# Five edits to a fused transformer kernel: DVE takes half of the modulation, one ada row moves into the MLP, four bias buffers, two score pairs ahead, ScalarE spreads the reciprocals

## The reference

```python
for i in range(2):
    mod = silu(c) @ ada_w[i] + ada_b[i]          # six rows of 1024: sh1, sc1, g1, sh2, sc2, g2
    mod_c = silu(c_ctx) @ ada_w[i] + ada_b[i]    # the same for the 256 context tokens
    h, hc = x * (1 + sc1) + sh1, ctx * (1 + sc1c) + sh1c
    y, yc = retention(h, hc) if i == 0 else neighbourhood(h, hc)
    x = layer_norm(alpha * x + g1 * y)           # ctx alike, in layer 0 only
    h = x * (1 + sc2) + sh2
    x = layer_norm(alpha * x + g2 * (relu(h @ mlp_w1[i]) ** 2 @ mlp_w2[i]))

# neighbourhood attention of layer 1: 32 heads of width 32, 256 queries, 256 local and 256 context keys
s = concat([q @ k_local.T + bias[head], q @ k_ctx.T])
o = softmax(s) @ v
```

## Time and profile before

| | us |
|---|---|
| median of three runs | 2924.24 |
| the profiled execution | 2926.24 |
| its span on the core | 2924.2 |
| PE busy in the span | 2752.2 (94%) |
| DVE busy | 1892.6 (65%) |
| ACT busy | 566.0 (19%) |
| POOL busy | 125.4 (4%) |

### The profile page before, as it was taken

One profiled execution on the slowest core, in us unless ns is written; L12 is line 12 of the kernel. 1 busy time (PEld: TensorE's weight loads), 2 busy tenths in 40 slices (PEclk: granted clock), 3 DMA queues, 4 the chain that ended last, 5 costly groups with the idle time before them and its releaser, 6 DMA issues.

```text
span 2924.2 us, 34915 instructions
## 1 busy us (share of the span) xinstructions
PE 2752.2 (94%) x13475; PEld 2209.9 (76%) x13475; DVE 1892.6 (65%) x2173; ACT 566.0 (19%) x1224; POOL 125.4 (4%) x118
## 2 busy tenths in 40 slices
PE   5999999799997997899899999999989999999998
PEld 3777776577776764789688877788878887878887
DVE  3455456455437357787776968587677687766766
ACT  2111110311111135212110231311020013131101
POOL 0000000000001002200000001010000000000100
PEclk8999999899998998999999999699999999978999
DMA  6332422344334443455454535155455454433643
GB/s 244 130 110 78 158 101 87 97 135 167 140 107 124 145 123 73 131 188 189 155 175 169 163 129 172 45 184 182 147 192 184 166 168 139 158 102 101 203 160 136
DMA packets 251850, 420.65 MB, mean 144 GB/s; under 512 B 35576, under 2 KB 93376, under 8 KB 251680
## 3 DMA queue, kind: packets, MB, share of 16 engines
q1 hardware_dynamic: 247824, 410.09, 42.9%
q0 software_dynamic: 2720, 5.14, 0.6%
q10 hardware_dynamic: 1136, 3.12, 0.3%
HBM read 417.27 MB, written 1.05 MB: 143 GB/s over the span
## 4 chain that ended last, share of the span: by engine, by line
PE 60%; issue 28%; DVE 5%; DMA 2%; POOL 2%; ACT 1%; SPq 1%; ACTq 0%; POOLq 0%; DVEq 0%
PE psum L406 57%; PE psum L420 2%; POOL small L1872 2%; DVE wgt_lo L1291 1%; SPq L1963 1%; DMA W<-nat_rpb 1%; DVE wgt_hi L1289 1%; DMA raw<-ada_w 1%; ACT psum L916 1%; ACT xh L916 0%; DMA raw<-nat_w_in 0%; DMA raw<-mlp_w 0%; POOL W L1912 0%; PE psum L627 0%; ACT W L916 0%
## 5 line engine op out<-in xcount | busy, mean ns | idle before, releaser
L1291 DVE TENSOR_TENSOR wgt_lo<-raw,wgt_hi 128x2048 fp32r<-128x2048 f32 (+2 forms) x352 | 776.1, 2205 | 12.1
L406 PE MATMUL psum<-wgt_hi,xh 128*128 128x512 f32 (+2 forms) x1824 | 704.3, 386 | 13.3 <-DVE wgt_lo L1291 8.0
L406 PE MATMUL psum<-wgt_lo,xh 128*128 128x512 f32 (+2 forms) x1824 | 695.3, 381 | 0.0
L406 PE MATMUL psum<-wgt_hi,xl 128*128 128x512 f32 (+2 forms) x1824 | 695.2, 381 | 0.0
L1289 DVE CAST wgt_hi<-raw 128x2048 fp32r<-128x2048 f32 (+2 forms) x352 | 415.5, 1180 | 334.2 <-PE psum L406 122.3
L406 PEld LDWEIGHTS psum<-wgt_hi,xh 128*128 128x128 f32 x1824 | 346.9, 190 | 93.1 <-issue 20.2
L406 PEld LDWEIGHTS psum<-wgt_hi,xl 128*128 128x128 f32 x1824 | 346.6, 190 | 66.5
L406 PEld LDWEIGHTS psum<-wgt_lo,xh 128*128 128x128 f32 x1824 | 346.8, 190 | 64.8 <-issue 1.0
L406 PE MATMUL psum<-wgt_hi,yh 128*128 128x512 f32 x944 | 371.8, 394 | 7.5 <-DVE wgt_lo L1291 4.9
L406 PE MATMUL psum<-wgt_hi,yl 128*128 128x512 f32 x944 | 367.8, 390 | 0.0
L406 PE MATMUL psum<-wgt_lo,yh 128*128 128x512 f32 x944 | 367.6, 389 | 0.0
(11 more groups left out here) (172 smaller groups left out, 2059.9 us busy)
## 6 DMA issues: line engine op xcount, KB each, us to landing
raw<-mlp_w SPq DMA_DIRECT2D x64, 1024.0 KB, 5.3
raw<-w_in SPq DMA_DIRECT2D x60, 1024.0 KB, 5.0
raw<-ada_w SPq DMA_DIRECT2D x48, 1024.0 KB, 7.3
raw<-ffn_w_gate SPq DMA_DIRECT2D x40, 1024.0 KB, 5.1
raw<-ffn_w_up SPq DMA_DIRECT2D x40, 1024.0 KB, 5.1
raw<-ffn_w_down SPq DMA_DIRECT2D x40, 1024.0 KB, 5.0
raw<-ret_w_in SPq DMA_DIRECT2D x24, 1024.0 KB, 5.3
raw<-nat_w_in SPq DMA_DIRECT2D x12, 1024.0 KB, 5.3
```

The costliest lines, as they stand in the source:

```text
L406: return pe.matmul(o, l, r, start=start_, stop=stop, skip_group_check=True)
L1291: v.tensor_tensor(wgt_lo[:, s % RING, :size], r, wgt_hi[:, s % RING, :size], ALU.subtract).then_inc(split_done.sem, split_done.up())
```

## The change

1. `low_x2` replaces `low_x` for `h0`, `h0m` and `h1`: DVE scales and shifts every odd tile in PSUM (two `tensor_scalar` of 128x256), ahead of the subtraction for the even tile before it; ACT only copies the odd tiles.
2. The four `ada_w` blocks of row 4 of layer 1 move from `nk` into the last chunk of the MLP of layer 0; those of row 5 move from `nv` to `nk`. The transposes that turn the rows into columns move along.
3. Four bias buffers in place of two. The two new ones lie in `x_rest`, which shares its memory with `xl`, so biases 2 and 3 are loaded after the last `nv` product; bias b from 4 on is loaded after the row minima of bias b-4.
4. Scores, row minimum and exponentials of pair 1 come before `nv` as well, like those of pair 0.
5. The reciprocals are still taken by DVE; ACT spreads them (`nat_spread`), after the exponentials of every fourth pair.

```diff
@@ PE, mlp()
+                    more_up, more_down = ({0: 0, 2: 1}, {2: 2, 3: 3}) if layer == 0 and c == 3 else ({}, {})
-                                       after=lambda b: b in in_up and modulation(1, c, in_up[b]),
+                                       after=lambda b: (b in in_up and modulation(1, c, in_up[b]), b in more_up and modulation(1, 4, more_up[b])),
...
+                    if more_up:
+                        modulation_columns(1, 4)
@@ PE, attention
-            features_by_tokens("nk", D, KT, 2 * T, "act", wb, after=lambda b: modulation(1, 4, b))
+            features_by_tokens("nk", D, KT, 2 * T, "act", wb, after=lambda b: modulation(1, 5, b))
             nat_scores(0)
-            tokens_by_features("nv", KT, 2 * D, D, range(4), x_op(xh), x_op(xl), "act", wb,
-                               after=lambda b: (modulation(1, 5, b), b == 0 and modulation_columns(1, 4)))
+            nat_scores(1)
             modulation_columns(1, 5)
+            tokens_by_features("nv", KT, 2 * D, D, range(4), x_op(xh), x_op(xl), "act", wb)
@@ ACT, operand_x()
-                    if streams == 2:
+                    if streams == 2 and kt % 2:
+                        act.wait_ge(affine_done.sem, affine_done.next())
+                        operand((name, kt), xh[:, kt, :])
+                    elif streams == 2:
@@ ACT, attention
+            def nat_spread(b):
+                act.wait_ge(recip_ready.sem, recip_ready.at(b + 1))
+                if b:
+                    act.wait_ge(psum_full.sem, filled(("no", b - 1)))
+                x = small[:, 256 + 8 * b:264 + 8 * b]
+                act_(n_inv.rearrange("p (h r) -> p h r", r=NAT_HD), x.unsqueeze(2).to_broadcast([P, 8, NAT_HD])).then_inc(inv_ready.sem, inv_ready.up())
@@ DVE
+            def affine_x(name, kt, layer, part):
+                dve.wait_ge(psum_full.sem, filled((name, kt)))
+                o = bank_of((name, kt))
+                for s in range(2):
+                    sc, sh = (mod[:, layer, part + j, kt, s:s + 1] for j in (1, 0))
+                    ins = v.tensor_scalar(o[:, s * T:(s + 1) * T], o[:, s * T:(s + 1) * T], sc, sh, ALU.mult, ALU.add)
+                ins.then_inc(affine_done.sem, affine_done.up())
+            def low_x2(name, layer, part):
+                for kt in range(KT):
+                    if kt % 2 == 0:
+                        affine_x(name, kt + 1, layer, part)
+                    low((name, kt), xl[:, kt, :], xh[:, kt, :], 1)
@@ SP
-                        sp.wait_ge(rowmin_ready.sem, rowmin_ready.at(4 * (b - 1)))
+                        if b < 4:
+                            sp.wait_ge(psum_full.sem, filled(("nv", 1, 3)))
+                        else:
+                            sp.wait_ge(rowmin_ready.sem, rowmin_ready.at(4 * (b - 3)))
```

More of the change, by code:

```diff
@@ L225, in build @@
         ln_in = signal("ln_in", 16)
-        bias_in = [signal(f"bias_in{s}", 16) for s in range(2)]
+        bias_in = [signal(f"bias_in{s}", 16) for s in range(4)]
         units = {}
@@ L322, in build @@
         nq, nk, nv = view(0, KT, T), view(2048, KT, 2 * T), view(6144, 4, D)
-        n_bias = [X[:, 2:4, :].rearrange("p a n -> p (a n)")[:, 0:1536].rearrange("p (h n) -> p h n", h=4), view(10752, 4, 384)]
+        n_bias = [X[:, 2:4, :].rearrange("p a n -> p (a n)")[:, 0:1536].rearrange("p (h n) -> p h n", h=4), view(10752, 4, 384)] + \
+            [x_rest[:, 0:6, :].rearrange("p a n -> p (a n)")[:, 1536 * k:1536 * (k + 1)].rearrange("p (h n) -> p h n", h=4) for k in range(2)]
         n_inv, n_out = W[:, 12288:12544], W[:, 12544:12800]
@@ L525, in mlp @@
                                        lambda k0, kn_, c0, cn: wblock(a["mlp_w2"][layer], c * KT + k0, kn_, c0, cn),
-                                       after=lambda b: b in in_down and modulation(1, c, in_down[b]),
+                                       after=lambda b: (b in in_down and modulation(1, c, in_down[b]), b in more_down and modulation(1, 4, more_down[b])),
                                        ready=lambda kt: (("up", layer), c * KT + kt))
@@ L652, in _ @@
             nat_scores(0)
[L653 to L654 removed]
+            nat_scores(1)
             modulation_columns(1, 5)
+            tokens_by_features("nv", KT, 2 * D, D, range(4), x_op(xh), x_op(xl), "act", wb)
             marks["nat"] = len(blocks) + RING
[L657 removed]
+            for n in range(2, N_PAIRS + 3):
                 if n < N_PAIRS:
                     nat_scores(n)
[L660 removed]
+                if n < N_PAIRS + 2:
                     nat_transposes(n - 2)
@@ L1073, in _ @@
                     act_(nv[:, tt, c * BANK:(c + 1) * BANK], bank_of(("nv", c, tt))).then_inc(act_out.sem, act_out.up())
[L1074 to L1077, removed]
+            for n in range(2, N_PAIRS + 2):
+                nat_turned(n - 2)
                 if n < N_PAIRS:
                     nat_exp(n)
+                if n % 4 == 0:
+                    nat_spread(n // 4 - 1)
             gates(1, 2, 1)
@@ L1399, in mlp @@
                         modulation(1, c)
+                    if layer == 0 and c == MLP_CHUNKS - 1:
+                        modulation(1, 4)
             v.memset(silc[:, 2 * KT:48], 0.0)
@@ L1414, in _ @@
             modulation(0, 1)
-            low_x("h0", range(4))
+            dve.wait_ge(mod_ready.sem, mod_ready.now())
+            low_x2("h0", 0, 0)
             prescale(range(4))
@@ L1496, in _ @@
                     add_and_norm(range(4), lambda c, tt: (("ry", h), c, tt), ("gate", 0, 2, 1, 1))
-            low_x("h0m", range(4))
+            dve.wait_ge(mod_ready.sem, mod_ready.now())
+            low_x2("h0m", 0, 3)
             prescale(range(4))
@@ L1500, in _ @@
             mlp(0, range(4))
-            low_x("h1", range(4))
+            dve.wait_ge(mod_ready.sem, mod_ready.now())
+            low_x2("h1", 1, 0)
             prescale(range(2))
@@ L1553, in _ @@
             nat_rowmin(0)
-            modulation(1, 4)
+            nat_rowmin(1)
+            modulation(1, 5)
             keep_up(("nv", 1, 3))
-            modulation(1, 5)
-            for n in range(1, N_PAIRS + 7):
+            for n in range(2, N_PAIRS + 7):
                 if n < N_PAIRS:
```

22 lines of the change are left out of this document (11 added, 11 removed).

## The result

The changed kernel took a median of **2894.54 us** (four runs, 2892.88 to 2898.25), against 2925.08 for the kernel before on the same chip: ratio 0.9897, 95% interval 0.9884 to 0.9910. The profiled execution took 2892.88, its span 2891.2 where before had 2924.2, so 33.0 us less; the prediction's sum was 33.2. That execution is the fastest of the four, and the profiled one of before was 2 us above its median; by the ratio the gain is 30.1 us. I go through it by stage.

What follows compares the result with a forecast made beforehand. PE, busy for 94% of the span, was taken as the bound, so gains need its waits or low clock. Terms -3.1 - 0.5 - 0.4 + 3.7 - 2.8 - 30.1 = -33.2 us gave 2891 us, own range 2882 to 2900.

Steps and rivals of the forecast that it cites:

- h0: Operands h0: the first split starts at 46.2 in place of 46.77; -0.5 us, bounds -1 and +1.
- h0m: Operands h0m before layer 0's MLP: the memset, SP's DMAs and PE's restart come earlier; -3.1 us.
- last MLP chunk: Layer 0's MLP: four ada blocks come in, three of them at 1.25 us each; +3.7 us, down to +3.2.
- h1: Operands h1: PE may come earlier by 0.9 us but must wait for the split; -0.4, bounds +1 and -2.
- nk and nv: nk unchanged; nv loses three ada blocks and one set of columns, with pair 1's scores and columns before it; -2.8 us.
- attention: End of nv to the gates: no wait for a bias remains, five periods of 11.29 us; 91.4 against 121.5, -30.1 us.
- for meetings of POOL's masks with DVE's cast I add 1.0: In the attention: allowance of 1.0 us for casts that take 2.21 us in place of 0.3 beside a mask.
- Rival (a): In the attention: mask and cast meet in every period, +11 to +20 us less the 1.0 counted; 2904 us, chance 0.10.
- (b): In the attention: waits did not make disturbed periods long; 15 us of the gain goes; 2906 us, chance 0.07.
- (c): In the attention loop: PE stays at 1.2 GHz, +9 us a period, +70 in all; 2963 us, chance 0.03.
- (d): Layer 0's last MLP chunk: weight blocks land in 11 us, seven late by 2.4 each, +17; 2908 us, chance 0.03.
- Rival (e): In the attention: four buffers change nothing, since biases 2 and 3 can't start before nv ends; 2914 us, chance 0.03.

Runs made afterwards that it cites:

- masks meet: The changed kernel with biases 4 to 7 issued two row minima later; 2894.72 us, ratio 0.9896 to the kernel before.
- masks apart: The changed kernel with biases 4 to 7 issued three row minima later; 2897.93 us, ratio 0.9902 to the kernel before.
- masks clear: The changed kernel with biases 4 to 7 issued four row minima later; 2889.84 us, ratio 0.9873 to the kernel before.
- four buffers only: The kernel before with the four bias buffers alone, all else as before; 2905.73 us, ratio 0.9927 to the kernel before.

## Why the prediction was right, step by step

| step | predicted | in the trace | what shows it |
|---|---|---|---|
| h0 | -0.5 | -0.7 | PE's first block 48.15 against 50.37, of which 1.5 is an earlier start of ACT (38.38 against 39.89) |
| h0m | -3.1 | -3.0 | ACT's first tile to memset 12.49 against 15.49; 3.1 over all kernels |
| restart and first chunk | 0 | +1.7 | DMA beside the bias 12.42 against 10.47, clock behind it |
| last MLP chunk | +3.7 | +3.7 | 87.53 against 83.85 |
| h1 | -0.4 | -0.1 | a DMA that landed later (12.80 us against 11.22) ate it |
| nk and nv | -2.8 | -2.8 | scores 0 to the end of nv, 46.1 against 48.9 |
| attention | -30.1 | -28.9 | 92.6 against 121.5 |
| outside the change | 0 | -2.9 | start -1.5, retention +0.3, after the attention -1.7 |
| sum | -33.2 | -33.0 | |

Two rows are not the change's. DVE's first split lies anywhere from 43.9 to 47.3 us, and last cast to end is 1739.8 to 1745.0, over the fourteen profiles; memset to restart varies by 2 us with the landing beside the bias. That spread is why kernels that differ by 3 us can't be told apart by time. The agreement of the two sums is therefore partly luck: without those rows the profile has -31.8 for what the prediction summed to -33.2, and the runs have -30.1. Two slips in its working matter little: for `nk` and `nv` its own -4.2 and +1.5 make -2.7, not -2.8, and PE sat idle for 9.6 us before its restart in the MLP, not some 8.

Within the attention the mechanism was right and two sizes were off. First, "**for meetings of POOL's masks with DVE's cast I add 1.0**": there was one, and it cost 2.8, since I priced only the lock and not the clock behind it (1.2 and 1.6 us). The five periods took 59.2 where I had 56.4 + 1.0. Second, the start-up: 19.0 where I had 20. The tail came out at 14.4 against 14.0.

One step left out a part of its effect: "**PE's row is full as well, so I take nothing**" for the spread on ACT. Its length is indeed free, but each DVE copy of this kind is open to the lock, and with the spread on DVE one of them made the start-up 2.6 us longer. In the kernel before none of the eight copies met a mask (0.29 us each); with four buffers two kernels had such meetings, three and two copies. I had the rule for the cast and did not apply it to the other copy.

Rival (a) claimed that mask and cast meet "either never or always". The runs showed once: until bias 6 SP is bound by its own issues, with masks 7.5 us apart, and the casts are 11.3 apart; and a met cast moves out of step. How many biases wait for a row minimum at all differs: bias 7 alone in the changed kernel, biases 6 and 7 in "masks meet", 5 to 7 in "masks apart", and all four in "masks clear". Rivals (b), (c) and (d) did not occur in the changed kernel; what (c) feared, a clock that stays low through the loop, did for 27.4 us with two buffers. Rival (e) is refuted by "four buffers only".

What carries the change, each undone in the changed kernel: four buffers 17.6 us timed, and by the stretches of the profiles the early pair 1 4.4, the operands 3.1, and the spread 2.6 in the start-up, where it met a mask; the ada rows, undone on top of the late pair 1, 2.5. The small ones rest on the profiles alone: the intervals of their timed ratios overlap.

## What to carry to other kernels

When two engines share a resource for the length of an instruction, count every instruction that is exposed to it, not the seconds it is busy: a 0.3 us copy on the wrong engine cost nine times its length, and issuing the other engine's input four pairs later saved 2.8 us. A buffer in hand removes the wait, and the fixed cost of issuing small DMAs is then the next bound: put them where the queue has slack, or between the loads. And read which parts of a difference lie outside the change before you call a sum confirmed.

## What the runs showed of the hardware

- **DVE's instruction waits for the whole of POOL's.** A DVE cast of 128x256 from SBUF to SBUF (0.29 us) and a copy of 128x8 spread to 128x256 (0.29) stood still while POOL's 128x1536 addition ran (3.45 us), and ended 0.15 to 0.16 us after it: 1.45, 2.59, 3.38 us for the cast and 3.14 and 3.53 for the copy, by how early they had begun. No cast and no copy of this kind that fell beside a mask in the attention kept its length, in any of the fourteen profiles. DVE instructions with a PSUM input beside a mask did: the bias subtraction (PSUM and SBUF in, 0.69) and the minimum (1.22). The Trainium skill, "SBUF — State Buffer", section "Who interferes with whom", says that a cast or copy in its two-port mode locks GpSimd out or is locked out for the whole instruction, and that an instruction with at most one SBUF input outside those modes is not; the traces agree on both counts, though they don't tell an instruction's mode.
- **A short wait of PE may or may not lower the clock.** Waits of 1.41 and 1.65 us left it at 1.00, waits of 1.31 and 1.52 were followed by scores of 1.92 and 2.07 us in place of 1.13, with 0.50 granted for 3.5 and 10.3 us. What decides is open.
- **Issuing the eight small DMAs of one bias costs SP 6.3 to 11.3 us**, and a weight block issued behind those of bias 0 or 1 landed in 10.2 to 12.8 us, where one alone took 5.1.
